# Decoder layer with product-key experts on one Trainium2 core: the last two weight splits are put behind the first expert gathers, and the table of interleaving counts is renumbered

## The reference

```python
q = (hf @ w_query).reshape(T, PEER_HEADS, 2, PEER_HALF)          # 1024 -> 2048 columns
s = jnp.einsum('thpd,pkd->thpk', q, sub_keys)                    # 2 x 128 scores per head
sv, si = lax.top_k(s, PEER_TOPK)                                 # top 16 of each half
cand = sv[:, :, 0, :, None] + sv[:, :, 1, None, :]               # pair sums
top_s, top_pos = lax.top_k(cand, PEER_TOPK)                      # 16 experts per head
idx, g = ..., jax.nn.softmax(top_s)                              # 8 x 16 = 128 experts per token
pre = jnp.einsum('td,thkd->thk', hb, down[ib])                   # one dot product per expert
out = jnp.einsum('thk,thkd->td', gb * jax.nn.gelu(pre), up[ib])  # weighted sum of rows of up
```

## Time and profile before

| | |
|---|---|
| median of three runs | 1802.55 us |
| profiled execution, its own time | 1803.89 us |
| its span, first to last instruction | 1801.9 us |
| PE busy | 1587.6 us (88%) |
| DVE busy | 1300.9 us (72%) |
| POOL busy | 666.5 us (37%) |
| ACT busy | 547.4 us (30%) |
| DMA, mean over the span | 276 GB/s |
| mean granted clock of PE | 0.952 |

### The profile page before, as it was taken

The page is one execution under the profiler, slowest core; times in us unless marked ns, Lnnn a source line. Parts: engine busy times, 40 slices in busy tenths (PEclk is TensorE's granted clock), DMA queues, the critical chain, the costliest instruction groups (busy, mean ns, idle before and its releaser), DMA issues.

```text
span 1801.9 us, 20598 instructions
## 1 busy us (share of the span) xinstructions
PE 1587.6 (88%) x7052; PEld 1171.4 (65%) x7052; DVE 1300.9 (72%) x2421; ACT 547.4 (30%) x1337; POOL 666.5 (37%) x533
## 2 busy tenths in 40 slices
PE   3998999988999799999997999997999998999900
PEld 2787877776777799888886888886444443444400
DVE  5766456666464598999997788898666656666698
ACT  2442234444722643111113788886000000000001
POOL 1000000000001565643556466666644445444572
PEclk8999999999999899999999999999999998999955
DMA  8423412133331433999999799999999999999994
GB/s 321 164 94 139 151 62 71 47 117 135 124 150 70 153 141 120 403 373 358 367 381 409 275 356 374 348 357 351 370 409 409 409 412 409 409 409 409 409 397 193
DMA packets 124231, 498.18 MB, mean 276 GB/s; under 512 B 13920, under 2 KB 14176, under 8 KB 113760
## 3 DMA queue, kind: packets, MB, share of 16 engines
q0 software_dynamic: 73728, 268.47, 38.6%
q1 hardware_dynamic: 50400, 228.41, 33.4%
HBM read 492.11 MB, written 4.72 MB: 276 GB/s over the span
## 4 chain that ended last, share of the span: by engine, by line
DVE 32%; PE 27%; DMA 26%; ACT 4%; issue 4%; POOL 3%; DVEq 3%; ACTq 1%; SPq 0%
DMA ring<-in_up,idx 20%; DVE ring L1464 7%; PE bank L759 5%; PE bank L494 5%; DVE accum L1673 5%; PE bank L496 5%; PE bank L495 5%; DMA ring<-in_down,idx 4%; POOL ring L1698 3%; PE bank L746 2%; DVE acc_ada L1122 2%; DMA raw<-in_ada 1%; DVE top_i L1486 1%; DVE top_i L1501 1%; DVE hot L1571 1%
## 5 line engine op out<-in xcount | busy, mean ns | idle before, releaser
L772 PE MATMUL bank<-stream,wmat 128*128 128x512 f32 x1024 | 444.9, 597 | 15.8 <-DMA stream<-in_up 8.3
L759 PE MATMUL bank<-h2T,stream 128*128 128x256 f32 x2048 | 452.5, 380 | 1.7 <-ACTq L1074 1.3
L1673 DVE SCALAR_TENSOR_TENSOR accum<-ring,share,accum 128x1024 f32<-128x1024 f32 x256 | 328.8, 1284 | 167.9 <-DMA ring<-in_up,idx 161.1
L759 PEld LDWEIGHTS bank<-h2T,stream 128*128 128x128 f32 x2048 | 385.9, 191 | 52.9 <-issue 1.7
L1698 POOL DMA_INDIRECT ring<-in_down,idx x256 | 323.8, 1265 | 245.0 <-DVE pre L1464 193.8
L772 PEld LDWEIGHTS bank<-stream,wmat 128*128 128x128 f32 x1024 | 196.3, 192 | 263.8 <-issue 246.9
L1698 POOL DMA_INDIRECT ring<-in_up,idx x256 | 263.1, 1028 | 233.6 <-DVE accum L1673 197.5
L1464 DVE CUSTOM_DVE_ANT_0 ring<-ring,h2row 128x1024 f32<-128x1024 f32 x256 | 305.8, 1218 | 42.7 <-DMA ring<-in_down,idx 37.3
L1708 POOL TENSOR_TENSOR wlo<-raw,whi 128x2048 fp32r<-128x2048 f32 x17 | 79.4, 4670 | 625.0 <-ACT whi L794 625.0
L494 PE MATMUL bank<-hT_hi,whi 128*128 128x512 f32 (+1 forms) x640 | 235.3, 368 | 22.9 <-DVE hT_lo L1175 12.5
L496 PE MATMUL bank<-hT_hi,wlo 128*128 128x512 f32 (+1 forms) x640 | 224.6, 351 | 0.0
(11 more groups left out here) (212 smaller groups left out, 1657.1 us busy)
## 6 DMA issues: line engine op xcount, KB each, us to landing
stream<-in_downT SPq DMA_DIRECT2D x128, 512.0 KB
stream<-in_up SPq DMA_DIRECT2D x128, 512.0 KB
raw<-in_ada SPq DMA_DIRECT2D x24, 1024.0 KB, 5.6
raw<-in_w_query SPq DMA_DIRECT2D x16, 1024.0 KB, 4.8
raw<-in_w_xp SPq DMA_DIRECT2D x4, 1024.0 KB, 6.0
raw<-in_w_gateA SPq DMA_DIRECT2D x4, 1024.0 KB, 4.7
raw<-in_w_branchP SPq DMA_DIRECT2D x4, 1024.0 KB, 4.8
raw<-in_w_q SPq DMA_DIRECT2D x4, 1024.0 KB, 4.8
```

What stands on the lines that cost most here:

```text
L759: last = pe.matmul(bank[:, 4 + i % 2, 0:DT], stream[:, i % RING, k * P:(k + 1) * P], h2T[:, k, GB * P:S], start=(k == 0), stop=(k == KT - 1))
L772: last = pe.matmul(bank[:, 2 * tb + half, :], wmat[:, i, tb * P:(tb + 1) * P], stream[:, (ET + i) % RING, half * S:(half + 1) * S], start= ...
L1673: dve.scalar_tensor_tensor(accum[:, b, :], ring[slot][:, :], share[:, b, k:k + 1], accum[:, b, :], ALU.mult, ALU.add).then_inc(sum_done, 1)
```

## The change

POOL makes `wlo` of the first 14 query chunks as before; that of query chunk 14 now follows the second gather, and that of query chunk 15 the fourth. The numbers of the interleaving are others: the exponentials and the transposes come ahead of other tiles, the routing holds dots at a smaller credit, fewer dots stand between softmax and one-hots, and an extra dot stands at every third tile number and not every second.

```diff
-EXP_AT = 70
-PICK_AT = 73
+EXP_AT = 66
+PICK_AT = 72
 DOTS_EXP = 4
 SPREAD_AT = 76
 STEP_DOTS = 2
-MORE_DOTS = 2
-DOTS_PICK = 14
-EARLY_DOTS = 119
-LATE_DOTS = 243
+MORE_DOTS = 3
+DOTS_PICK = 8
+EARLY_DOTS = 125
+LATE_DOTS = 242
 POOLED = 16
-ROUTE_PER_DOT = 1.1
+POOL_FIRST = 14
+POOL_MORE = 2
+ROUTE_PER_DOT = 0.985
...
             for n in POOL_CHUNKS:
-                wlo_make(n)
+                if n < QUERY + POOL_FIRST:
+                    wlo_make(n)
             for g in range(GB * P):
                 b, k = g // P, g % P
...
                 gather(down, b, k, down_slot[g])
+                late = QUERY + POOL_FIRST + (g + 1) // POOL_MORE - 1
+                if (g + 1) % POOL_MORE == 0 and late < len(CHUNKS):
+                    wlo_make(late)
```

## The result

The changed kernel takes 1818.26 us, the median of four runs (1817.63 to 1821.27), against 1801.17 us for the kernel before in its four. The ratio is 1.0099, with a 95% interval of 1.0080 to 1.0117: slower by 17 us. The prediction had the sign and a third of the size; 1818.26 lies above its range of 1798 to 1816. The profiled execution after took 1818.49 us on its own, 14.6 us above that of before; what follows accounts for those 14.6 us. The other 2.5 us of the 17 lie in the choice of executions: the profiled one of the kernel before was the slowest of its four (1803.89 us against a median of 1801.17).

What follows compares the result with a forecast made beforehand. No single engine bounds the whole; DMA limits the up stage, whose start follows PE. Terms 18.9 + 3.5 - 11.8 - 3.0 - 3.5 + 1.3 = 5.4 us gave 1808.0 us on the median, range 1798 to 1816.

Steps and rivals of the forecast that it cites:

- step 3: ACT's exponentials ahead of tile 66: PE stands still 3.5 us at tile 68, bounds 0 to 14.4 us.
- step 2: Routing on DVE: with added dots at 1.15 us each it ends at 969.4 instead of 958.58, bounds 963.5 to 980.3.
- step 6: Up stage: one dot more is left for it, costing 1.3 us, bounds 0 to 2.0 us.
- signs of being wrong: PE leaves the query by 722, routing ends before 964 or after 975, or up stage starts before 1258.
- Step 1: Query: PE waits 15.9 us for chunk 14's split and loses 3.0 us of clock; down stage starts 18.9 us later.
- Step 4: First quads: the old 11.77 us pause at tile 76 goes, saving 3.0 us of clock; first quad at 1003.9.
- Step 5: Last 52 down tiles: fewer waits of PE for DVE save 3.5 us, so the up stage starts 4.1 us later.
- dots held up by DMA: Rival, chance 0.17 shared with late indices: dots go at 1.81 us, lengthening the wait at tile 66; 1817 us.
- No wait at tile 66: Rival, chance 0.25: routing ends at 966 or before, step 3 is zero, the sum 1.9 us; 1804.4 us.
- late indices: Rival, chance 0.17 shared with slow dots: first gather stays at 715, down stage starts 27.8 us later; 1817 us.
- faster: Rival, chance 0.18: the old pause and the lag at the end outweigh the query's new pause; 1797.5 us.

Runs made afterwards that it cites:

- The exponentials at tile 70: Changed kernel with the exponentials back ahead of ACT's tile 70 and the transposes ahead of tile 73: 1804.62 us, 1.0023 of the kernel before.
- The slot experiments: Up gathers through the ring from slot 4 on: changed kernel 1.0080, changed kernel with exponentials at tile 70 1.0003, kernel before 0.9986.
- the order with fitted numbers: Kernel before with POOL's new order, exponentials ahead of tile 66 and transposes ahead of tile 72, old dot counts and credit: 1.0051, again 1.0036.
- the order alone: Kernel before with only POOL's new order of the splits, all numbers as before: 1811.27 us, 1.0056; again 1809.77 us, 1.0057.

## Why the prediction was wrong

The signs and the chain of events were right; the sum was 5.4 us and came out at 14.6 us in the profile. Two terms of the sum were mis-sized above all, the wait at tile 68 (step 3, with the late routing of step 2 and the clock behind it) and the handover to the up gathers (step 6). None of the prediction's own signs of being wrong came up: PE left the query at 729.87, the routing ended by 972.4, and the up stage started after 1258. By its steps:

- **Step 1** held. First gather 706.00 for 706.14, first split's end 712.90 for 713.4, PE's pause of 16.4 us, start of the down stage 729.87 for 731.4: the clock cost 2.4 us and not 3.0, the splits were 0.5 us earlier, and chunk 15's old wait of 0.46 us was gone.
- **Step 2** was 3.0 us short. The first piece of the routing ended at 738.0 (737.4 forecast). The other 11 added dots then cost 15.1 us, 1.37 each and not 1.15. Of the 2.4 us too much, 1.31 are one wait for a gather at 750.32; the rest is spread over small gaps and slightly longer instructions, for which the trace names no cause. The exponentials start at 972.42, not 969.4.
- **Step 3 failed, and it is the step that decides.** "PE stands still for 3.5 us" was 10.34 us. 3.2 us of the 6.8 come from a later restart, nearly all of it step 2: tile 68 restarts at 975.19 and not 972.0. The other 3.6 us are on PE's side, which reached the tile earlier: tile 67 ended at 964.86, not 968.5. Of that, 1.5 us are from step 1, and 2.1 us are time that PE had lost in its first down tiles before and that the forecast carried along in the old 956.6. Before, 68 tiles took 237.1 us, with waits of 1.28 us (for ACT) and 0.41 us (for the stream) near 731 and 739; now they take 235.0 us, 3.456 us a tile without a wait. Those 3.6 us did not cost time, since they only made a wait longer. What costs is that the wait existed, and 3.2 us of it above the estimate. The exponentials at tile 70 show the step's whole price: 12 us in the profiles, 14 us by the ratios. The forecast took the tile number as given and asked only how long PE would wait there.
- **Step 4** had the cover right (DVE idled for 13.8 us there). The first quad came at 1008.91 and not 1003.9: 3.2 us of it are step 3, and 1.6 us are the slower clock behind the new wait (33.5 us for nine tiles and the transposes, for 31.9 by 3.456 us a tile and 0.8 us for the transposes), which the sum left out though it had charged exactly this for the other pauses. The saving of 3.0 us of clock was also too high: the second quad waits for ACT's second set of one-hots, which the old pause had hidden, so only 0.9 us came back.
- **Step 5** gave 4.3 us for 3.5.
- **Step 6 failed.** "One dot more" was 1.3 us and came out at 4.2. The new counts also shift the ring slots: the first up gather uses slot 0, whose last dot is now number 254 and not 253 (counted from 0 to 255), and POOL idles 6.7 us longer. The slot experiments show 5.0 and 3.1 us of sums for it in the changed kernel (exponentials at 66 and at 70) and 0.9 us in the one before.

Added up, against the forecast of 5.4: routing +3.0, clock behind the new wait +1.6, second quad +2.1, the last tiles -0.8, handover +2.9, rounding +0.4, together 14.6 us.

Of the rivals, the late routing ("dots held up by DMA", 1817 us) was nearest in number. Its mechanism was partly there (1.37 us a dot, not 1.81). "No wait at tile 66" was false (10.34 us), "late indices" was false (first gather at 706.00), and "faster" was false: even the order with fitted numbers is at 1.0036.

One thing stays open: that last kernel, in which neither DVE waits for exponentials nor PE for the first one-hots, is still slower, by 0.24 to 0.48% in its second set of runs. Its first quad is 4.0 us later than that of the kernel before in one profile, while its sums are 0.8 us shorter. The pause in the query is then not fully absorbed, since tile 76 ends only at about 427 on the table's scale, 4 us after the old pause ended. The parts agree: the down stage starts 17.8 us later, of which the old pause takes up 11.8 and the old loss in the first tiles 2.1, and 3.9 are left, near the 4.1 us that the prediction's own sum left over. The up stage starts 4.1 us later too. That fits most of the 5.3 us between the medians, but no run takes the pause away at these numbers.

## What to carry to other kernels

Where engines meet at fixed step numbers, a pause of one engine is not a term to be added: first find which of the meeting points is late afterwards, and move its number. When a count changes, follow everything that is derived from it, ring slots included, to the instruction that waits for the slot. A dot moved out of a late stage into an earlier one is only worth what the earlier stage's end does not wait for.

## What the runs showed of the hardware

A two-input DVE instruction that met a POOL subtraction showed the wait inside its own length: dots of 3.53 and 4.02 us for 1.23. In the earlier trace rows the same happened to other instructions, and the prediction had counted it where it saved time and where it cost time. New was the clock behind waits: PE's 10.34 us at tile 68 cost 1.6 us more over the next nine tiles, its 16.40 us in the query 2.4 us, and where DVE let it wait 11.77 us, 3.0 us. With the order alone a wait of only 4.72 us was followed by 16 small matmuls in 3.57 us for 1.78 and a tile in 3.84 us for 3.46, 2.2 us in all; so the cost did not follow the length of the wait here. The granted clock of the whole span hardly shows it (0.948 in the profile of the changed kernel, 0.952 before); that of short stretches does, as 975 to 978 us in the changed kernel:

```profile
975.00:978.00 3.00, 2.81 (x7) 2.30 (x8) 2.85 (x8) 0.41 (x2) 2.69 (x2) 0.50 0.96 350
978.00:981.00 3.00, 3.00 (x15) 2.60 (x14) 2.56 (x11) 0.39 (x1) 1.97 (x3) 0.94 0.88 320
```

The order of the columns is that of the earlier trace rows.
